# Modulation sums in the feed-forward stages: transposes on TensorE and a free-axis sum on VectorE in place of products with a column of ones

## The reference, cut to what matters

```python
c_act = jax.nn.silu(c)
for layer in range(DEPTH):
    mod = (c_act @ ada_w[layer] + ada_b[layer]).reshape(bsz, N_SUB, 3, D_MODEL)[:, :, :, None, :]
    def modulate(t, sub):
        return rms_norm_2(t, norm_g[layer, sub]) * (1.0 + mod[:, sub, 1]) + mod[:, sub, 0]
    h = modulate(x, 0)
    x = x + HALF_STEP * (1.0 + mod[:, 0, 2]) * swiglu(h, ffn_w_gate[layer, 0], ffn_w_up[layer, 0], ffn_w_down[layer, 0])
```

## Time and profile before

| | |
|---|---|
| time, median of 3 runs | 2418.38 us (2417.86 to 2418.47) |
| span of the profiled execution | 2415.9 us |
| median less span | 2.5 us |
| TensorE matmuls busy | 2251.3 us (93%) |
| VectorE busy | 1721.0 us (71%) |
| ScalarE busy | 1174.9 us (49%) |
| DMA, mean | 209 GB/s |
| granted TensorE clock, mean | 0.962 |

### The profile page before, as it was taken

How to read it: one execution, slowest core, us unless ns; L and a number is a source line. 1 busy time by engine, 2 the same in 40 slices (tenths; PEclk the granted TensorE clock), 3 DMA queues, 4 the chain that set the end, 5 groups by cost and what they waited for, 6 DMA issues and landing times.

```text
span 2415.9 us, 33624 instructions
## 1 busy us (share of the span) xinstructions
PE 2251.3 (93%) x13722; PEld 1991.7 (82%) x13722; DVE 1721.0 (71%) x2093; ACT 1174.9 (49%) x1358; POOL 233.1 (10%) x182
## 2 busy tenths in 40 slices
PE   7789999998779999997999989899999999898998
PEld 7668888888568888886998977699989988767997
DVE  4766679994767679997867685777677766476554
ACT  3554356884453346884334663343343344434333
POOL 5100312212000302310000011000000020000000
PEclk9989999998889999998999999999999999998999
DMA  9128778993117779995885322388668743305652
GB/s 248 53 93 305 257 267 322 359 358 145 53 41 284 249 256 329 363 352 197 294 279 184 141 95 102 136 286 279 219 238 293 261 141 130 122 1 183 209 174 70
DMA packets 241449, 505.55 MB, mean 209 GB/s; under 512 B 10383, under 2 KB 104529, under 8 KB 241296
## 3 DMA queue, kind: packets, MB, share of 16 engines
q1 hardware_dynamic: 216144, 417.84, 49.6%
q10 hardware_dynamic: 21600, 77.09, 8.9%
q0 software_dynamic: 3552, 8.47, 1.4%
HBM read 502.31 MB, written 1.05 MB: 208 GB/s over the span
## 4 chain that ended last, share of the span: by engine, by line
PE 59%; DVE 10%; ACT 3%; issue 1%; ACTq 0%; DVEq 0%
PE PS L1051 21%; PE PS L1067 10%; PE PS L894 6%; PE PS L1143 5%; PE PS L852 4%; DVE WGL L2280 2%; PE PS L1242 2%; PE PS L1262 2%; PE PS L1152 1%; PE PS L1306 1%; DVE AR L2283 1%; ACT WGH L1724 1%; PE PS L1109 1%; DVE AR L2280 1%; DVE XN L2280 1%
## 5 line engine op out<-in xcount | busy, mean ns | idle before, releaser
L2280 DVE TENSOR_TENSOR WGL<-ring,WGH 128x2048 fp32r<-128x2048 f32 x258 | 592.2, 2302 | 250.4 <-ACT WGH L1724 136.3
L1051 PE MATMUL PS<-XTB,WGH 128*128 128x256 f32 x2816 | 517.3, 286 | 4.9 <-DVE XTB L2280 4.7
L1051 PEld LDWEIGHTS PS<-XTB,WGH 128*128 128x128 f32 x2816 | 449.1, 194 | 15.1 <-issue 8.1
L1051 PE MATMUL PS<-XTB,WGL 128*128 128x256 f32 x1408 | 401.3, 285 | 0.0
L1051 PEld LDWEIGHTS PS<-XTB,WGL 128*128 128x128 f32 x1408 | 272.6, 194 | 0.0
L2280 DVE TENSOR_TENSOR WDL<-ring,WDH 128x1024 fp32r<-128x1024 f32 (+1 forms) x136 | 217.0, 1596 | 34.7 <-ACT WDH L1881 22.8
L1881 ACT ACTIVATE WGH<-ring 128x2048 fp32r<-128x2048 f32 x96 | 183.3, 1913 | 113.5 <-PE PS L1143 39.3
L894 PE MATMUL PS<-XTB,WGH 128*128 128x256 f32 (+1 forms) x1104 | 214.3, 296 | 21.3 <-DVE WGL L2280 18.7
L1724 ACT ACTIVATE WGH<-ring 128x2048 fp32r<-128x2048 f32 (+1 forms) x74 | 138.8, 1878 | 181.8 <-PE PS L894 59.9
L894 PEld LDWEIGHTS PS<-XTB,WGH 128*128 128x128 f32 (+1 forms) x1104 | 178.7, 198 | 33.7 <-DVE WGL L2280 21.1
L1923 ACT ACTIVATE XN<-PS 128x256 f32<-128x256 f32 x88 | 33.7, 383 | 355.0 <-PE PS L1051 323.7
(11 more groups left out here) (503 smaller groups left out, 4488.3 us busy)
## 6 DMA issues: line engine op xcount, KB each, us to landing
FA<-in_ada_w ACTq DMA_DIRECT2D x144, 512.0 KB, 6.1
ring<-in_moe_w_up SPq DMA_DIRECT2D x64, 1024.0 KB, 7.1
ring<-in_moe_w_gate SPq DMA_DIRECT2D x64, 1024.0 KB, 8.1
ring<-in_moe_w_down SPq DMA_DIRECT2D x64, 1024.0 KB, 7.7
ring<-in_ffn_w_gate SPq DMA_DIRECT2D x44, 1024.0 KB, 5.9
ring<-in_ffn_w_up SPq DMA_DIRECT2D x44, 1024.0 KB, 9.5
ring<-in_ffn_w_down SPq DMA_DIRECT2D x44, 1024.0 KB, 7.3
ring<-in_hyb_w_in SPq DMA_DIRECT2D x10, 1152.0 KB, 6.7
```

The lines of the kernel that those rows point to most:

```text
L1051: ins = mm(PS[:, 4 + b, m * T:(m + 1) * T], w_[:, b, w], x_[:, k, :], start=k == 0 and q == 0, stop=k == KD - 1 and q == 2)
L2280: return V.tensor_tensor(out_, x_, y_, op)
```

## The change

In the loop of the feed-forward stages `mod_sums` gives way to `sums_by_token`: eight fp32 transposes of the same eight blocks of `ADC`, with the identity `ID`, into 128 x 1024 of PSUM banks 6 and 7 (the old sums wrote 8 columns of bank 6). Its waits are the same two. One step later VectorE waits for them, reduces the 128 x 8 x 128 values along their last axis into the 8 columns `M8` (in the tile ST) with a TENSOR_REDUCE and waits for its end, and `mod_out` adds the bias from there. Nine of the 18 turns take the new way: three in each of ffn00, ffn01 and ffn10. The sums in the expert stages and in `last_sums` stay as they were.

```diff
@@ PE, hidden_layer
-                        mod_sums(turn + j // 5, PS[:, 6, 0:AW // P])
+                        sums_by_token(turn + j // 5)
@@ PE
+            def sums_by_token(turn):
+
+                pe.wait_ge(S("mod_acc"), TURN * (turn + 1))
+                pe.wait_ge(S("mod_out"), turn)
+                for m in range(AW // P):
+                    ins = nc.tensor.transpose(PS[:, 6 + m // 4, m % 4 * P:(m % 4 + 1) * P], ADC[:, m * P:(m + 1) * P], ID)
+                ins.then_inc(S("mod_ps"), 1)
@@ DVE, hidden_layer
                     if turn is not None and j % 5 == 0 and 5 <= j <= 15:
-                        mod_out(turn + j // 5 - 1, PS[:, 6, 0:AW // P])
+                        done = turn + j // 5 - 1
+                        dve.wait_ge(S("mod_ps"), done + 1)
+                        c(V.tensor_reduce(M8[:, 0:AW // P], PS[:, 6:8, :].rearrange("p b (m n) -> p (b m) n", n=P),
+                                          AX.X, ALU.add))
+                        mod_out(done, M8[:, 0:AW // P])
```

## The result

The changed kernel took 2407.7 us (median of 4, 2405.1 to 2408.3), against 2418.4 for the kernel before: a ratio of 0.9947, with a 95% interval from 0.9933 to 0.9961. That ratio makes 2405.6 of the 2418.4, which is 1 us under the range; the median of the four itself, 2407.7, lies within it. Two further sets of timings gave 0.9956 [0.9939, 0.9972] and 0.9963 [0.9948, 0.9977]. Over the timings that were taken beside the other kernels the kernel before has a mean of 2419.1 us (82 timings, 2414.3 to 2426.0; with before_again, before_third and before_fourth 2419.2 over 95), and the changed one 2408.2 us (16 timings, 2401.5 to 2413.8): 10.9 us less, with a standard error of 0.9. The forecast was 8.3 us less. So direction and size were near, and some 2.6 us of the gain were not in the sum.

A forecast was written before the change was run, and what follows sets the result against it. The prediction took TensorE's stream to bound the three loops: nine turns at 0.92 us save 8.3 us, the reduction and stage heads add nothing, so 2418.4 - 8.3 = 2410.1 us. The range was 2406.5 to 2415.5.

The forecast's parts named there:

- What bounds the loops: In the three changed loops TensorE is busy throughout, so a microsecond off its stream is one off the stage.
- The burst: On TensorE in the loops, eight transposes take 0.79 us where the old sums took 1.71, saving 0.92 us a turn.
- The reduction at nothing: In the loops, VectorE's added 1.3 us a turn is covered by its idle time and costs nothing.
- the term for the stage heads: At the heads of later stages, slow clock stretches may fall differently: taken at zero, 3.4 us either way.
- the span: The profiled execution: 2415.9 us would become 2407.6, with the 2.5 us around it unchanged.
- Rival 1: At later stages' heads, three more slow stretches give back 5.1 us, leaving 3.2 us saved, 2415.2; chance 0.15.
- Rival 2: In the loops, nine transpose bursts bring the clock down, losing 15.3 us, 2425.4; chance 0.03.
- Rival 3: In the loops, VectorE's 1.3 us reach TensorE every turn, 11.7 us in all, 2421.8; chance 0.03.
- Rival 4: In the loop bursts, transposes of ADC are no cheaper than the sums, so the time stays 2418.4; chance 0.04.

The follow-up runs named there:

- before_again: The kernel before, unchanged, profiled a second time; with its other two repeats and all other timings, mean 2419.2 us over 95 timings.
- before_third: The kernel before, unchanged, profiled a third time; with its other repeats and all other timings, mean 2419.2 us over 95 timings.
- before_fourth: The kernel before, unchanged, profiled a fourth time; with its other repeats and all other timings, mean 2419.2 us over 95 timings.
- transposes_alone: The changed kernel without the VectorE reduction, bias added to 8 columns of the transposed block; ratio 0.9961, median 2408.2 us.
- reduction_alone: The kernel before with its old sums, plus the VectorE reduction of banks 6 and 7, result unused; ratio 0.9999, median 2418.2 us.
- matmul_128: The changed kernel with ordinary fp32 matmuls by the identity in place of the transposes, two instructions a block; ratio 1.0003.
- only_ffn00: The kernel before with the change in ffn00's three turns only; ratio 0.9972, mean 6.7 us less than before.
- the two with the filler: The changed kernel with two unused fp32 matmuls of 512 columns behind the last sums of ffn00, ffn01 and ffn10, run twice; ratios 0.9949 and 0.9953.
- only_ffn10: The kernel before with the change in ffn10 only; ratio 0.9993, mean 1.3 us less than before.
- one_block: The kernel before with one of eight blocks summed in each of the nine loop bursts, 2 instructions in place of 16; ratio 0.9927.
- double_sums: The kernel before with each of the nine loop bursts issued twice, 32 instructions in place of 16; ratio 1.0116, median 2448.0 us.

## Why the prediction was wrong, point by point

**What bounds the loops: right.** TensorE is busy throughout, before and after, and nothing it waits for became late.

**The burst: right.** 0.79 us for 0.79, from a row of another stage with the same form. The distance of two turns (1166.27 and 1209.63 in the trace of after, 1166.12 and 1210.43 before) went from 44.31 to 43.36 us, where 43.4 was forecast. The Trainium skill's figure ("TensorE: Matmul & The Clock Gate", Part 4) of some 275 ns for a 128x128 transpose in a kernel's context is given there for bf16. The duration of one fp32 transpose in this trace, 272 ns, is near it; eight durations would be 2.2 us, and the burst of eight costs 0.79 us.

**The reduction at nothing: right.** 1.22 us as worked out from the smaller reductions, and no cost, shown from both sides by transposes_alone and reduction_alone.

**The step that failed: the term for the stage heads, taken at zero with 3.4 us either way.** From ffn00's first product on, the four executions of before average 1298.0 us and the three of after 1287.6: 10.4 us less, which fits the 10.9 of the timings. By pieces (means of the table's columns before rounding):

| piece | before | after | difference |
|---|---|---|---|
| the three loops | 570.2 | 561.5 | -8.7 |
| hyb | 254.1 | 251.6 | -2.5 |
| between ffn01 and ffn10 | 14.4 | 14.6 | +0.2 |
| mlstm | 259.4 | 260.2 | +0.8 |
| ffn11 and the rest | 199.9 | 199.7 | -0.2 |

The loops hold the forecast 8.3 and 0.4 more. Most of the 0.4 is the clock too: in before_fourth a slow stretch reaches some 4 us into ffn01's and ffn10's loops, which last 190.5 and 190.4 us there, and the other three executions alone give 569.9 for the three loops, 8.4 more than after. The heads and mixers, taken at nothing, gave 1.7 us on top: 2.5 in hyb less 0.8 in mlstm, and the 0.8 is within the scatter of mlstm's three executions. What the sum had at nothing is the time that TensorE's work spends at the lower clock, 34.1, 27.3, 34.1 and 29.8 us in hyb's stretch before and 23.9 in all three executions after. A further 0.3 us lies around the span, which the forecast left at 2.5 us unchanged: time less span is on average 2.1 us before and 1.8 after. Together that is 2.4 of the 2.6 us. The allowance of 3.4 us either way was about the right size for the shift of the mean. What it lacked was the spread of single executions, 12 us in the kernel before, and of the ratio, whose interval alone is 3.4 to 4 us each way on a few timings; the low end of the range, 2406.5, left out the lower part of that, and the first ratio, which stands for 12.8 us less where all timings together show 10.9, fell 1 us below. That it fell outside and not just inside is chance; the 2.6 us by which all timings miss the forecast, with a standard error of 0.9, hardly are. The three timings of before agreed within 0.6 us and I took this for the kernel's spread.

**Rival 1** (a part is given back at the heads) has the right place and the wrong sign in hyb; in mlstm it was so in two of three executions (261.3 and 261.4) and not in the third. **Rival 2** (transposes bring the clock down) did not occur: the three loops are at 1.00. What brought it down in these loops was the other form, one-column products, when the burst was twice as long. **Rival 3** (VectorE's 1.3 us reach TensorE) is excluded by transposes_alone. **Rival 4** is excluded by the burst, and matmul_128 shows what it would have looked like.

**What stays open.** With all three turns of ffn00 changed, hyb's stretch is 251.5 to 251.8 us in seven of seven profiles (after three times, transposes_alone, only_ffn00 and the two with the filler), and without it, 252.2 to 255.6 in seven others: the four of before, only_ffn10, reduction_alone and matmul_128, all with 16 instructions a burst in ffn00. So the shorter stretch goes with the change in ffn00. That it is shorter because ffn00 ends earlier is not shown: one_block, whose ffn00 loop is 4.9 us shorter, has 253.3, and double_sums, whose loop is 11.4 us longer, has 252.1. Why its length jumps between 252.2 and 255.6 in executions of one kernel, and why mlstm's does between 258.0 and 261.4, is shown only as far as the share of work at the lower clock. I could not fix when a slow stretch begins, so that the loops' end and its place were never varied one without the other.

## What to carry to other kernels

A small fp32 matmul used for a sum over partitions was paid by the instruction here, two for each at 0.107 us, so a transpose (one instruction) and a free-axis sum on an engine with idle time can be cheaper, although it writes 128 times as much. Take the price of a burst from start to start in a stage that already has the same form, and then ask which waits of the other engines cover their part. An edit that shifts the end of a TensorE-bound loop by some microseconds can move the stages behind it by a like amount through where the clock's slow stretches fall: put that in the range, and take the spread from many timings, since three can agree by chance.

## What the runs showed of the hardware that I had not expected

A burst of 32 fp32 MATMUL instructions with one moving column, 3.4 us of gapless work at full clock, brought the granted clock of 1.2 GHz for 3.4 or 6.8 us at eight of nine places, in loops that are at 2.4 GHz between them; a burst of 16 (1.7 us) did so nowhere in the loops of the profiled executions. So doubling nine bursts of 1.7 us cost 31.7 us in the three loops and not 15.4. And 16 fp32 MATMUL instructions of 128 columns take as long (1.70 us) as 16 of one column (1.71 us).
